# A fused encoder block on one core: every expert's rows moved as 128 with a bound, and the down product in three passes

## The reference, cut to what matters

```python
def body(y, args):
    tok_b, g_b, e_b = args
    xb = hf[tok_b]
    u = jax.nn.silu(xb @ w_gate[e_b]) * (xb @ w_up[e_b])
    yb = (u @ w_down[e_b]) * g_b[:, None]
    return y.at[tok_b].add(yb), None
...
shared = (jax.nn.silu(hf @ ws_gate) * (hf @ ws_up)) @ ws_down
return (routed + shared).reshape(B, S, D)
```

## Time and profile before

| what | value |
|---|---|
| median of 3 runs | 1127.55 us (1127.16 to 1128.62) |
| the profiled execution | 1132.51 us, of which 1130.7 us are the profile's span |
| PE, DVE, ACT, POOL busy | 92%, 74%, 46%, 21% of the span |
| stage of the experts | from about 395 us to the end |
| DMA queues of weight: q1 (SP) | 259.12 MB |
| q0 (POOL's gathers and adds) | 34.62 MB |

### The profile page before, as it was taken

The page is one execution under the profiler, slowest core; times in us unless marked ns, Lnnn a source line. Parts: engine busy times, 40 slices in busy tenths (PEclk is TensorE's granted clock), DMA queues, the critical chain, the costliest instruction groups (busy, mean ns, idle before and its releaser), DMA issues.

```text
span 1130.7 us, 16022 instructions
## 1 busy us (share of the span) xinstructions
PE 1037.0 (92%) x4777; PEld 733.0 (65%) x4778; DVE 836.9 (74%) x1480; ACT 521.8 (46%) x610; POOL 234.5 (21%) x145
## 2 busy tenths in 40 slices
PE   1899997978998989999998999999999999899995
PEld 1898887657446447766775666667766666566662
DVE  4887899886665457787876787778787776676865
ACT  3425463364111145555554554555555454545542
POOL 0000000100000034353321323423222222342210
PEclk9899998989996999999999999999999999999998
DMA  9775300600948078999999999999999999999944
GB/s 358 244 277 178 101 1 1 229 14 13 388 186 327 27 249 269 356 344 343 338 366 348 323 333 344 345 337 329 324 338 333 346 308 339 304 328 334 340 113 152
DMA packets 82999, 297.60 MB, mean 263 GB/s; under 512 B 10799, under 2 KB 23131, under 8 KB 73437
## 3 DMA queue, kind: packets, MB, share of 16 engines
q1 hardware_dynamic: 69188, 259.12, 63.6%
q0 software_dynamic: 12208, 34.62, 13.4%
q10 hardware_dynamic: 1514, 2.97, 0.7%
HBM read 274.71 MB, written 24.12 MB: 264 GB/s over the span
## 4 chain that ended last, share of the span: by engine, by line
DMA 37%; PE 13%; issue 7%; POOLq 3%; DVE 3%; SPq 2%; ACT 1%; POOL 0%; DVEq 0%; ACTq 0%
DMA y_rows<-yb,row_numbers 28%; PE ps L2034 6%; DMA side<-in_w_exp_up 5%; PE ps L2089 4%; DMA main<-in_w_exp_up 2%; POOLq L1757 2%; DMA xg<-h_rows,row_numbers 1%; SPq L1573 1%; PE ps L2024 1%; PE ps L2134 1%; POOLq L1751 1%; ACT w_gate_up_hi L1802 1%; DVE main L2008 0%; DVE w_gate_up_lo L1901 0%; DVE pick L1881 0%
## 5 line engine op out<-in xcount | busy, mean ns | idle before, releaser
L1901 DVE TENSOR_TENSOR w_gate_up_lo<-side,w_gate_up_hi 128x2048 fp32r<-128x2048 f32 x64 | 146.8, 2294 | 78.9 <-ACT w_gate_up_hi L1802 78.8
L1901 DVE TENSOR_TENSOR w_gate_up_lo<-main,w_gate_up_hi 128x2048 fp32r<-128x2048 f32 x64 | 146.7, 2292 | 71.9 <-ACT w_gate_up_hi L1802 71.8
L1594 POOL DMA_INDIRECT y_rows<-yb,row_numbers x62 | 116.2, 1874 | 375.3 <-issue 311.4
L1802 ACT ACTIVATE w_gate_up_hi<-side 128x2048 fp32r<-128x2048 f32 x64 | 122.1, 1910 | 95.5 <-DMA side<-in_w_exp_up 54.1
L1802 ACT ACTIVATE w_gate_up_hi<-main 128x2048 fp32r<-128x2048 f32 x64 | 122.2, 1910 | 91.5 <-PE ps L2034 45.8
L2034 PE MATMUL ps<-w_gate_up_hi,xT_hi 128*128 128x512 f32 x512 | 144.7, 404 | 11.8 <-DVE xT_lo L1905 8.7
L2034 PE MATMUL ps<-w_gate_up_hi,xT_lo 128*128 128x512 f32 x512 | 137.6, 390 | 0.0
L2034 PE MATMUL ps<-w_gate_up_lo,xT_hi 128*128 128x512 f32 x512 | 137.3, 390 | 0.0
L2034 PEld LDWEIGHTS ps<-w_gate_up_hi,xT_hi 128*128 128x128 f32 x512 | 91.4, 189 | 32.1 <-issue 14.2
L2034 PEld LDWEIGHTS ps<-w_gate_up_hi,xT_lo 128*128 128x128 f32 x512 | 96.2, 188 | 21.1
L2034 PEld LDWEIGHTS ps<-w_gate_up_lo,xT_hi 128*128 128x128 f32 x512 | 96.1, 188 | 21.0
(11 more groups left out here) (309 smaller groups left out, 1554.9 us busy)
## 6 DMA issues: line engine op xcount, KB each, us to landing
side<-in_w_exp_gate SPq DMA_DIRECT2D x60, 512.0 KB, 9.6
side<-in_w_exp_up SPq DMA_DIRECT2D x60, 512.0 KB, 23.9
main<-in_w_exp_gate SPq DMA_DIRECT2D x60, 512.0 KB, 9.9
main<-in_w_exp_up SPq DMA_DIRECT2D x60, 512.0 KB, 24.6
side<-in_w_ada SPq DMA_DIRECT2D x20, 1024.0 KB, 7.7
main<-in_w_exp_down SPq DMA_DIRECT2D x16, 1024.0 KB, 23.1
maskb<-in_w_exp_down SPq DMA_DIRECT2D x16, 1024.0 KB, 20.4
side<-in_w_exp_down SPq DMA_DIRECT2D x16, 1024.0 KB, 23.6
```

The source lines that it names most:

```text
L1594: return pool.indirect_dma_start(out=G.y_sums, out_offset=bass.IndirectOffsetOnAxis(ap=sidx[0:rows, n:n + 1], axis=0), in_=yb[0:rows, slot ...
L1802: nc.scalar.activation(whi[:, half], wgu[n % RING][:, :, HALF * half:HALF * (half + 1), :] .rearrange("p m c f -> p c m f"), ACT.Copy).the ...
L1901: nc.vector.tensor_tensor(wlo[:, half], src, whi[:, half].bitcast(F32), ALU.subtract).then_inc(s_wlo, 1)
```

## The change

Four things change, all for the experts.

1. The tree and the count table go. Gather and add always name 128 rows, with `bounds_check=SEQ - 1` in both; the numbers of empty places lie beyond the bound, so that their rows aren't moved.
2. `build_pick` compares with a table `K_RANK` in place of 0..127. The token of rank r in its expert no longer sits in partition r but in the one whose table entry is r: partitions 0 to 7 have ranks that are multiples of 16, partitions 8 to 15 those plus 1, and so on, so that each group of eight partitions has the same number of tokens to within one. The comparison becomes one instruction of 512 columns.
3. The down product is done in three float32r passes like gate and up, 12 matmuls in place of 4. For it ACT writes the high parts of the transposed u and of the down weights (one buffer each), DVE the low parts; the low part of the weights goes over the weights themselves.
4. The result's 1024 columns are all copied by ACT, none by DVE.

```diff
+    slot = np.arange(P)
+    turn = 4 * ((slot >> 2 ^ slot >> 5) & 1) + (slot & 3)
+    k[:, K_W:K_W + P] = 16 * turn + (slot >> 3)
...
+        def add_rows(pool, slot, n):
+
+            return pool.indirect_dma_start(out=G.y_sums, out_offset=bass.IndirectOffsetOnAxis(ap=sidx[:, n:n + 1], axis=0),
+                                           in_=yb[:, slot, :], in_offset=None, compute_op=ALU.add,
+                                           bounds_check=SEQ - 1, oob_is_err=False)
...
                         pool.wait_ge(s_xp, e + 1)
                         pool.sem_inc(s_passed, 1)
-                        count = count_of(e + AHEAD)
-                        by_size(count, SIZES, lambda rows: gather_rows(pool, n % RING, (n + AHEAD) % UNROLL, rows).then_inc(s_g[n % RING], 16))
+                        gather_rows(pool, n % RING, (n + AHEAD) % UNROLL).then_inc(s_g[n % RING], 16)
                     if ahead(2):
                         pool.wait_ge(s_ya, e + 2)
-                        pool.wait_ge(s_yd, e + 2)
                         pool.wait_ge(s_sc, SC0 + 16 * e)
                         pool.sem_inc(s_passed, 1)
-                        count = count_of(e)
-                        by_size(count, SIZES, lambda rows: add_rows(pool, n % 2, n, rows).then_inc(s_sc, 16))
+                        add_rows(pool, n % 2, n).then_inc(s_sc, 16)
...
+                def uT_high(e, slot):
+                    act.wait_ge(s_ut, e + 1)
+                    nc.scalar.activation(uhi[:, :, :], ps[:, 2 + slot, 0:FC * P].rearrange("p (f t) -> p f t", f=FC), ACT.Copy).then_inc(s_uTh, 1)
+
+                def high_down(t, n):
+                    act.wait_ge(s_wd[n % RING], 16 * (UNROLL // RING * t + n // RING) + 16)
+                    if not (isinstance(t, int) and t == 0 and n == 0):
+                        act.wait_ge(s_dn, UNROLL * t + n)
+                    nc.scalar.activation(wdh[:, :, :], wd[n % RING], ACT.Copy).then_inc(s_wdh, 1)
...
-                    nc.scalar.activation(yb[:, n % 2, 0:512], ps[0:CAP, 4, :], ACT.Copy,
+                    nc.scalar.activation(yb[:, n % 2, :].rearrange("p (a b) -> p a b", a=2), ps[0:CAP, 4:6, :], ACT.Copy,
                                          scale=found[:, n, 1:2]).then_inc(s_ya, 1)
+                    if ahead(1):
+                        uT_high(e + 1, (n + 1) % 2)
+                        high_down(t, n + 1)
...
+                def low_down(e, slot):
+                    dve.wait_ge(s_wdh, e + 1)
+                    nc.vector.tensor_tensor(wdl[slot][:, :, :], wd[slot], wdh[:, :, :].bitcast(F32), ALU.subtract).then_inc(s_wdl, 1)
...
-                    pe.wait_ge(s_wd[n % RING], 16 * ((UNROLL // RING) * t + (n // RING + 1)))
+                    pe.wait_ge(s_wdl, e + 1)
...
                         for f in range(FC):
-                            ins = nc.tensor.matmul(ps[0:CAP, 4 + half, :], uT[:, n % 2, f, :],
-                                                   wd[n % RING][:, f, 512 * half:512 * (half + 1)], start=f == 0, stop=f == FC - 1)
+                            for j, (up, wp) in enumerate(((uhi, wdh), (ulo, wdh), (uhi, wdl[n % RING]))):
+                                ins = nc.tensor.matmul(ps[0:CAP, 4 + half, :], up[:, f, :], wp[:, f, 512 * half:512 * (half + 1)],
+                                                       start=f == 0 and j == 0, stop=f == FC - 1 and j == 2)
```

More of the change, by code:

```diff
@@ L48 @@
 STEPS = (SEQ - 1) // CAP
-MEAN = SEQ * 8 // E_N
-SIZES = [*range(MEAN - 16, CAP, 8), CAP]
 QK_W = 2 * HEADS * DH
@@ L85 @@
 K_W = K_SINI + NT * ROT_I
+K_RANK = K_SEL
 def constants():
-    k = np.zeros((P, K_W), np.float32)
+    k = np.zeros((P, K_W + P), np.float32)
     i = np.arange(P)
@@ L1584, in pick_rows, with gather_rows @@
             return nc.vector.scalar_tensor_tensor(sidx[:, n:n + 1], f, -1.0, pad[:, 0:1], ALU.add, ALU.add)
[L1586 to L1589 removed]
+        def gather_rows(pool, slot, n):
+            return pool.indirect_dma_start(out=xg[slot], out_offset=None, in_=G.h2_rows,
+                                           in_offset=bass.IndirectOffsetOnAxis(ap=sidx[:, n:n + 1], axis=0),
                                            bounds_check=SEQ - 1, oob_is_err=False)
[L1592 to L1595 removed]
+        def add_rows(pool, slot, n):
+            return pool.indirect_dma_start(out=G.y_sums, out_offset=bass.IndirectOffsetOnAxis(ap=sidx[:, n:n + 1], axis=0),
+                                           in_=yb[:, slot, :], in_offset=None, compute_op=ALU.add,
+                                           bounds_check=SEQ - 1, oob_is_err=False)
         with ExitStack() as inner:
@@ L1743, in _ @@
                 pool.wait_ge(s_yw, 16 * NT)
-                def by_size(count, sizes, move):
-                    if len(sizes) == 1:
-                        move(sizes[0])
-                        return
-                    half = len(sizes) // 2
-                    with pool.If(count > sizes[half - 1]):
-                        by_size(count, sizes[half:], move)
-                    with pool.Else():
-                        by_size(count, sizes[:half], move)
-                def count_of(e):
-                    return pool.value_load(G.count_tab[0:1, bass.ds(e, 1)], min_val=0, max_val=SEQ)
                 def step(t, n, ahead):
@@ L1838, in _ @@
                 high_half(0, 1, 1)
+                uT_high(0, 0)
+                act.wait_ge(s_sdn, NT)
+                high_down(0, 0)
                 def step(t, n, ahead):
@@ L1879, in build_pick @@
                 def build_pick(e, slot):
-                    for i in range(NT):
-                        ins = nc.vector.tensor_scalar(pick[:, slot, i, :], k[:, K_IOTA:K_IOTA + CAP],
-                                                      posm[:, bass.ds(NT * e + i, 1)], None, ALU.is_equal)
-                    ins.then_inc(s_pick, 1)
+                    full = [P, NT, CAP]
+                    place_of = posm[:, bass.ds(NT * e, NT)].rearrange("p (i o) -> p i o", o=1).broadcast_to(full)
+                    iota = k[:, K_RANK:K_RANK + CAP].rearrange("p (o t) -> p o t", o=1).broadcast_to(full)
+                    nc.vector.tensor_tensor(pick[:, slot], iota, place_of, ALU.is_equal).then_inc(s_pick, 1)
                 def read_found(e, n):
@@ L2187, in build @@
                                                                                G.rows[:, 1:3, :].rearrange("p i d -> p (i d)"))]
+        G.w_down_hi = nc.alloc_sbuf_tensor_at("w_down_hi", [P, FC, D], FR, offset=main_at + 4 * (G.QKC + 2048))
+        G.w_down_lo = [nc.alloc_sbuf_tensor_at(f"w_down_lo{n}", [P, FC, D], FR, offset=at)
+                       for n, at in enumerate((side_at + 4 * 8192, main_at + 4 * G.QKC, maskb_at, rows_at + 4 * D))]
         G.held = [ExitStack(), ExitStack()]
```

46 lines of the change are left out of this document (21 added, 25 removed).

## The result

The changed kernel takes 1080.8 us (median of 4 runs, 1076.4 to 1102.4) beside 1128.1 us before in the same round: ratio 0.956, 95% interval 0.953 to 0.960. One of the four executions, 1102.4 us, counts as slow; without it the median is 1079.8. The profiled execution took 1076.4 us with a span of 1074.6.

A forecast was written before the change was run, and what follows sets the result against it. The prediction took the loads to set the end: rate -24.4, spare rows -3, empty places +12, end of stage +2.6, together -12.8 us from a profiled 1132.51 us; median forecast 1114 us, range 1100 to 1136.

The forecast's parts named there:

- The bound of the kernel before: Experts' stage: computing sets the pace early, loads late; the loads set the end, at 10.6 to 11.4 us an expert.
- the size of the rate's return: Loads from 600 to 1070: the rate holds at 347 GB/s in place of 329, 24.4 us less.
- more is had: Rival: empty places nearly free and the last load's long tail gone, -25 us, 1102 us; chance 0.16.
- the computing's part: Middle of the experts' stage: computing needs 9.5 to 10.2 us an expert, under the loads' 10.6; costs and gains nothing.
- The adds' loop: POOL: 0.3 us replaces the tree between adds, the loop falls from 10.28 to about 8.5 us, worth nothing by itself.
- The cause of the fall in rate: Late loads: work spread unevenly over 16 engines, by code packets or row counts that don't divide by 16.
- Empty places: Gathers and adds: some 7500 more empty places at 26 ns each, over 16 engines +12 us; bounds 0 and 24.
- The term of 3 us for spare rows: POOL's queue: about 258 spare rows go, 1.06 MB, 3 us less at 347 GB/s.
- The end of the stage: Last down product: the new wait lies bare, +4.1 us; three products ahead gain 0.5 each; net +2.6 us.

The follow-up runs named there:

- h1: The kernel before with odd experts' adds put into a second sum with its own semaphore, left out of the output: 1141.7 us.
- e1: The kernel before with the changed moves alone (128 rows, bound, rank table, no tree or counts), down product still plain float32: 1101.5 us.
- h4: The changed kernel without VectorE's step for empty places and with odd experts' adds in a second sum, left out of the output: 1073.4 us.
- e3: The changed kernel with the count and tree of branches put back, each leaf the same move of 128 rows: 1142.4 us.
- e5: The kernel before with each row count rounded up to a multiple of 16 in place of 8: 1129.0 us.
- h2: e3 with odd experts' adds put into a second sum with its own semaphore: 1088.4 us.
- h3: The changed kernel with odd experts' adds put into a second sum with its own semaphore: 1081.2 us.
- j1: h1 with the tree kept, but each leaf the same move of 128 rows with rank table and bound: 1104.7 us.
- e9: e3 with the wait for the add before moved into the leaves, so that POOL walks the tree while that add lands: 1123.1 us.
- e4: The changed kernel with places in plain order (0 to 127) in place of the rank table: 1170.7 us.
- f3: e1 with gathers and adds over 112 rows in place of 128, evenly spread by a table of its own: 1102.4 us.
- e7: The changed kernel with 85 more plain POOL instructions per expert, ahead of the gather's wait: 1127.7 us.
- f1: The changed kernel with 32 plain POOL instructions between the wait for the add before and the add: 1183.3 us.
- f2: The changed kernel with 32 plain POOL instructions ahead of the wait for the gather's row numbers: 1098.3 us.
- g1: The changed kernel without VectorE's step that gives an empty place its row number: 1084.7 us.

## Why the prediction was wrong, step by step

*The bound of the kernel before* was half read. The loads were one: h1, where no add waits for the one before it, gains nothing. But the chain of adds stood beside them. The prediction read it from one pair of adds as 10.28 us, "as long as TensorE's period"; the mean of 51 is 8.74 + 2.09 = 10.83 us, the kernel's whole pace, and nearly every add waited for the landing. "On the path of the loads that is worth nothing by itself" holds only while the loads bind as well.

*The step that failed is the size of the rate's return.* For the moves the sum had -24.4 - 3 + 12 = -15.4 us, and they gave 29.0 (e1). The prediction took the best stretch of before, 347 GB/s, as the loads' own pace, 10.6 us an expert, and gave back 24.4 us. But that stretch had the same rounded moves in it. With equal rows the loads keep up with 9.71 us an expert at 378 GB/s (h4), and no engine waits for weights in e1, h4 or the changed kernel. The term should have been open upward; the rival "more is had" had the direction but took 25 us from the same 347.

*Therefore the computing's part was not free.* "All of this part costs and gains nothing in the middle; its cover is the loads": the cover went, and this part, forecast at +2.6 us, gave 20.7 (e1 to the changed kernel). The paces themselves were nearly right: TensorE 9.5 forecast, 9.71 in h4; ScalarE 8.4, and 168.60 of 200 us busy is 8.3 at 9.84 an expert; VectorE 9.35 and at most 9.8, and 195.10 of 200 is 9.6. Expected were 9.5 to 10.2 us an expert in all, and 9.84 it is.

*The adds' loop* was priced at nothing, which is true only while something as long stands beside it. Left in the changed kernel, the tree would cost 61 us (e3). The 0.3 us put in the tree's place are at least 0.86 in the trace and 1.19 in the mean, and the loop takes 9.87 us, not 8.5.

*The cause of the fall in rate* was half right. Divisibility by 16 (e5) is refuted. Instruction packets do go with a late engine: in h2, whose loads have no slack, the last one is 14.1 us late at 58 packets, in h3 0.4 at 4. They don't always: it is 2.2 us late in j1 at 56 and 0.3 in e3 at 53. And the tree with its packets is worth 7 us there (h2 to h3), and 3 in the kernel before (j1 to e1, which differ in the second sum too). The rule on code fetches in the Trainium skill (Runtime: NRT & Kernel Launch, Instruction fetch mechanics) foretold that these packets would go, and the traces agree: 48 from 440 to 1000 before, 4 after. What costs 37 us are the rounded moves (h1 to j1).

*Empty places* were priced at 26 ns, 12 us in all. A packet of 4 or 8 bytes on POOL's queue takes 9 ns on average in the changed kernel, 4.2 us by the same working, and since the loads don't bind, nothing is seen of it. The term of 3 us for spare rows had its bytes right.

*The end of the stage* cost more than forecast. The last down product was to come 6.1 us after the one before had ended and to be over after 9.0; it comes after 5.6 (1044.14 - 1038.54) and is over after 10.2 (1048.78 - 1038.54), against 4.9 before. After the wait its matmuls start 0.43 us apart (0.23 in the product before it), at a granted clock of 0.50, the lower level of 1.2 GHz, from 1044.1 to 1047.5:

```profile
1044.14 0.80 PE L2097 MATMUL ps<-w_down_hi,uT_hi 128*128 128x512 f32 x1 [5.37 <-DVE w_down_lo L1925]
1044.73 0.63 PE L2097 MATMUL ps<-w_down_hi,uT_lo 128*128 128x512 f32 x1
```

Open stay two things: how the rounded moves' 37 us divide between changing size, places in order and spare rows; and why an add lands 0.7 us later when POOL walks its tree meanwhile (e9). No run takes the rounded moves alone out of the kernel before and leaves tree and chain.

## What to carry to other kernels

A transfer rate read from a busy stretch is a lower bound of what the engines can do, not a floor for the next version: ask what the change removes from that very stretch. Where several loops have almost one period (here 10.9, 10.8 and 10.2 us), list them all; a change that shortens one gives nothing and one that shortens all can give more than the sum of the single ones, so price it by the slowest loop left, and read each loop as a mean of many turns. In this kernel, with half of the places full, indirect DMAs of a fixed 128 rows, with a bound and with the full places spread over the partitions, are cheaper than ones cut to the count; without the spreading the kernel was slower than with the cut ones (e4).

## What the runs showed of the hardware

- A place that the bound rejects costs about 9 ns of one engine: the changed kernel's POOL queue has 9050 packets of 4 or 8 bytes from 440 to 1000, 9 ns in the mean. A 4 KB row costs some 160 ns gathered or 327 added.
- Some 64 rows in the first partitions of 128 take an add 10.37 us to land (e4), spread over all 8.68 us (the changed kernel).
- Moves of 112 rows have row packets of 263 ns on average (f3), of 128 rows 247 (e1). The number of rows is not all: with 128 rows it was 262 in e7 and 302 in f1.
- An add landed later where a gather was issued within some 4.5 us behind it in f2 (9.24 us against 8.68 in the changed kernel) and in one stretch of g1 (9.38 against 8.53). It is no rule: in e1 (4.32 us behind) it landed in 8.73, in f1 (4.08) in 8.33.
- Plain semaphore increments of POOL follow each other every 78 ns (f1, f2, e7).
